# Eight changes of order and of PSUM banks at TensorE's waiting places in a two-block transformer kernel

## The chip, the cores and the metric

One NeuronCore of a Trainium2 chip runs the whole program. The metric is the time on the device in microseconds (us), the median of several executions; the profile is one further execution, taken by the hardware profiler. TensorE (PE) multiplies, VectorE (DVE), ScalarE (ACT) and GpSimd (POOL) work on tiles in SBUF (the first two also on PSUM, where PE writes), SyncE (SP) issues most of the transfers.

## The reference

256 tokens of width 1024 in float32 go through two transformer blocks. The first has a conditioning (six vectors of 1024 from `silu(c) @ w_ada`, with a bias), one attention that keeps the best keys of an indexer, one stick-breaking attention, and a layer of experts of which all 16384 rows of `u` and `v` are read. The second has a mixer of a short convolution, a block attention and a gated linear attention (GLA), a cross attention to a memory of 256 tokens, and a gated feed-forward layer of width 2752. Cut to what the change touches:

```python
mod = (cond @ w_ada[l] + b_ada[l]).reshape(b, 6, d)
shift1, scale1, gate1, shift2, scale2, gate2 = [mod[:, i] for i in range(6)]
hn = modulate(rmsnorm(x, norm1_g[l]), shift1, scale1)
...
suffix = lax.cumsum(log_one_minus, axis=3, reverse=True) - log_one_minus
a = jnp.where(strict, jnp.exp(log_beta + suffix), 0.0).astype(v.dtype)
...
hn2 = modulate(rmsnorm(x, norm2_g[l]), shift2, scale2)
f = peer_ffn(hn2.reshape(b * s, d), peer_wq[l], peer_sub_keys[l], peer_u[l], peer_v[l]).reshape(b, s, d)
x = x + gate2[:, None, :] * f
```

## The kernel before

The weights pass once through the core in **units** of 128 x 1024 floats (512 KB), in the order that `stream_plan` writes down (L204 on): w_ada (raw, for the conditioning), w_qi to w_vb, then w_qa to w_pb with a w_ada unit behind each, w_pa, w_o, w_pq, 128 units of u, 128 of v, and the second block's w2_*, w_up and w_dn. SyncE fetches them into 13 slots. ScalarE copies a unit's high half (`split`, L1298, type fp32r), and VectorE (L1834) or GpSimd (L2625) makes the low half, the rest to float32; `on_pool` in `stream_plan` says which of the two. A product takes three matmuls (`mm3`): high by high, high by low, low by high. There are three to eight buffers for split units, so an engine can be ahead of PE by two to six units, and every wait is a semaphore.

Each engine has a program of its own in the same order (`tensor_program`, `scalar_program`, `vector_program`, `gpsimd_program`). The products are `lin` (blocks of two column tiles in one bank, all steps of the first column before the second, unless `both`), `lin_nat` and `one`. Work that runs beside the products is a generator in `jobs`: each call of `unit` takes one step (one `yield`) of the first three jobs left, and `jobs.finish()` runs all that is left at once. All engines must keep to the same order of steps.

A PSUM bank is taken by `claim(b)`, which waits for the semaphore in `freed[b]`, that is for its last reader. `block_banks` hands out the banks of products, and `attention_banks` those of scores ("s") and transposes ("t").

- **Conditioning.** VectorE adds the w_ada units up in `ada_acc` (L1866, L1869), a group of 8 units for each of the six vectors. `ada_total` on PE then sums over the partitions with one-column matmuls, in bank 6 but for the second group, and `mod_part` on VectorE (L1850) adds the bias. It is called at the first w_ada unit after a group is complete, on both engines; the third group is gate1, which w_o needs, and the sixth is summed behind `total(1)`, ahead of w_pq.
- **Stick-breaking attention** (`stick_steps`): two waves of four heads; the cumulative sums are products with a triangle of ones, in banks 6, 7, 6, 7. VectorE adds them (L2125), and GpSimd masks before (L2702) and after (L2707). The value products take banks 6 and 7.
- **Attention** (`attend`): scores of two items at a step, soft maxima on VectorE (L1970, L1973) and ScalarE (L1412), transposes on PE (L787) in the same bank as the item's scores, values in banks 2 and 3. Scores of items 2 and 3 are issued one step ahead of the transposes of items 0 and 1, into the same banks 4 and 5.
- **Router.** After each block of w_pq (banks 4, 5, 6; the first is in bank 6) `key_scores` is a job of two steps. `jobs.finish()` ends the list behind the last block.
- **v stage.** Beside it the memory's normalisation (L1920, L1390, L2652) goes as a job, and the coefficients are made by ScalarE (L1637) and VectorE (L2373).
- **Second block.** w2_lr (the 16 columns of the gate) comes behind w2_mv and the start of the second attention; GLA's steps start behind it and wait for its copy (ScalarE, L1317). GpSimd makes the low halves of the normalised tiles (L2652), and takes its share of low halves of units only after them.
- **w_dn.** `lin` with 22 steps for each column; step k waits for `f_lo` k + 1, the low half of act_t (L2594).

## Time and profile before

| | us |
|---|---|
| median of 3 runs | 1443.64 |
| lowest and highest | 1441.86, 1446.01 |
| span of the profiled execution | 1450.8 |
| its PE busy | 1402.9 (97%) |
| its VectorE busy | 1097.6 (76%) |
| its ScalarE busy | 836.6 (58%) |
| its GpSimd busy | 358.2 (25%) |

The span is that from the first to the last instruction of the profiled execution; nothing that the profile shows lies outside it, and no other time of that execution is given, so the span stands for it, 7.2 us above the median. A matmul's end in the profile is modelled: matmuls overlap, so a busy PE can still be one that runs at half clock. So both are to be read: the idle time before an instruction, in brackets with the engine and line that ended it, and the granted clock (PEclk, a share of 2.4 GHz; 0.5 is 1.2 GHz).

### The profile page before, as it was taken

The page shows a single profiled execution, that of the slowest core. Times are in us where ns is not written, and L with a number is a line of the kernel's source. Part 1 is how long each engine was busy: PE and PEld are TensorE (multiplying, and loading weights), DVE is VectorE, ACT ScalarE, POOL GpSimd, SP SyncE. Part 2 cuts the span into 40 slices and gives each one's busy share as a digit, 9 for nine tenths or more (in the row PEclk, how much of TensorE's full clock was granted, in tenths as well). Part 3 has the DMA queues.
Part 4 walks back from the last instruction along what each step waited for, and adds up shares of the span by engine and source line. Part 5 has one row for each costly group of instructions (what it writes and reads, how often), then busy time and mean ns, then how long its engine had stood idle before and what let it go on. Part 6 is the DMA issues. An engine that isn't in the chain of part 4 may idle for free.

```text
span 1450.8 us, 25879 instructions
## 1 busy us (share of the span) xinstructions
PE 1402.9 (97%) x10406; PEld 1303.3 (90%) x10406; DVE 1097.6 (76%) x1903; ACT 836.6 (58%) x1447; POOL 358.2 (25%) x227
## 2 busy tenths in 40 slices
PE   7999999899999999999999999999999999899997
PEld 5998899799999999999988888887889899799997
DVE  6788887467889888999766666777667667787762
ACT  3554774444454577777654454465446666766651
POOL 3216101234345100000032322344322221433200
PEclk9999999999999999999999999999999999999999
DMA  9757775445655444444456666665666535275530
GB/s 383 270 187 268 248 240 176 160 150 187 187 182 162 155 151 148 148 150 148 146 188 220 196 192 193 217 191 183 190 205 244 180 115 189 81 252 177 191 116 30
DMA packets 73721, 268.24 MB, mean 185 GB/s; under 512 B 8401, under 2 KB 9730, under 8 KB 72834
## 3 DMA queue, kind: packets, MB, share of 16 engines
q1 hardware_dynamic: 71280, 256.41, 54.0%
q10 hardware_dynamic: 1426, 7.56, 1.5%
q0 software_dynamic: 896, 2.62, 0.5%
q8 instruction: 83, 1.36, 0.4%
q14 instruction: 36, 0.29, 0.1%
HBM read 262.88 MB, written 3.67 MB: 184 GB/s over the span
## 4 chain that ended last, share of the span: by engine, by line
PE 80%; DVE 13%; ACT 4%; DMA 1%; POOL 1%; issue 1%; DVEq 0%; ACTq 0%; POOLq 0%
PE bank L611 79%; DVE split L1834 3%; DVE ada_acc L1869 2%; DVE PR L2284 1%; DVE PR L2281 1%; ACT split L1298 1%; DMA ringb<-in_w_ada 1%; DVE PR L2289 1%; POOL H L2652 0%; DVE rT L1920 0%; PE bank L787 0%; POOL split L2625 0%; DMA vecs<-in_vecs 0%; DVE H L2373 0%; DVE PA L2085 0%
## 5 line engine op out<-in xcount | busy, mean ns | idle before, releaser
L611 PE MATMUL bank<-H,split 128*128 128x256 f32 x5928 | 736.3, 283 | 17.1 <-DVE split L1834 7.1
L611 PEld LDWEIGHTS bank<-H,split 128*128 128x128 f32 x5928 | 713.8, 190 | 24.1 <-DVE split L1834 9.4
L1298 ACT CAST split<-ringb 128x1024 fp32r<-128x1024 f32 x350 | 365.8, 1047 | 288.6 <-PE bank L611 278.4
L611 PE MATMUL bank<-split,H 128*128 128x512 f32 (+1 forms) x1728 | 390.9, 387 | 1.7 <-POOL split L2625 1.5
L2625 POOL TENSOR_TENSOR split<-ringb,split 128x1024 fp32r<-128x1024 f32 x91 | 225.4, 2478 | 670.4 <-ACT split L1298 670.4
L1834 DVE TENSOR_TENSOR split<-ringb,split 128x1024 fp32r<-128x1024 f32 x259 | 327.6, 1268 | 77.7 <-ACT split L1298 77.5
L611 PEld LDWEIGHTS bank<-split,H 128*128 128x128 f32 x1728 | 320.9, 188 | 69.8 <-POOL split L2625 2.5
L2373 DVE TENSOR_TENSOR H<-PR,H 128x256 fp32r<-128x256 f32 x128 | 137.3, 1074 | 106.3 <-ACT H L1637 106.2
L1834 DVE TENSOR_TENSOR split<-far,split 128x1024 fp32r<-128x1024 f32 x77 | 99.8, 1304 | 33.4 <-ACT split L1298 33.2
L1298 ACT CAST split<-far 128x1024 fp32r<-128x1024 f32 x89 | 92.9, 1047 | 53.2 <-PE bank L611 44.0
L1613 ACT ACTIVATE PR<-bank 128x512 f32<-128x512 f32 (+31 forms) x59 | 28.6, 486 | 75.9 <-PE bank L611 75.9
L2639 POOL TENSOR_TENSOR rT<-rT 128x256 f32<-128x256 f32 x25 | 26.7, 1067 | 177.2 <-ACT rT L1347 175.6
L611 PE MATMUL bank<-act_t,split 128*128 128x256 f32 x528 | 60.3, 276 | 0.8 <-DVE act_t L2594 0.8
L611 PEld LDWEIGHTS bank<-act_t,split 128*128 128x128 f32 x528 | 60.0, 188 | 1.0 <-DVE act_t L2594 1.0
L1596 ACT ACTIVATE xT<-cst,rT 128x128 bf16<-128x128 f32 x168 | 55.7, 438 | 0.0
L1637 ACT CAST H<-PR 128x256 fp32r<-128x256 f32 x128 | 51.2, 400 | 0.6 <-PE bank L611 0.6
L2346 DVE TENSOR_TENSOR PR<-bank,PR 128x224 f32<-128x224 f32 (+31 forms) x64 | 33.3, 520 | 23.6 <-PE bank L611 23.3
L2336 DVE TENSOR_TENSOR xT<-rt,cpw 128x512 bf16<-128x512 bf16 x126 | 45.8, 418 | 0.0
L2625 POOL TENSOR_TENSOR split<-far,split 128x1024 fp32r<-128x1024 f32 x12 | 31.1, 2591 | 58.5 <-ACT split L1298 58.5
L611 PE MATMUL bank<-Ym,split 128*128 128x256 f32 x336 | 41.2, 281 | 1.5 <-DVE Ym L1995 1.5
L611 PEld LDWEIGHTS bank<-Ym,split 128*128 128x128 f32 x336 | 39.7, 188 | 2.4 <-DVE split L1834 1.7
L611 PE MATMUL bank<-xT 128*128 128x128 bf16 x504 | 36.2, 219 | 0.0
(298 smaller groups left out, 1265.0 us busy)
## 6 DMA issues: line engine op xcount, KB each, us to landing
ringb<-in_u SPq DMA_DIRECT2D x128, 512.0 KB, 3.6
ringb<-in_v SPq DMA_DIRECT2D x128, 512.0 KB, 4.2
ringb<-in_w_ada SPq DMA_DIRECT2D x28, 512.0 KB, 5.3
far<-in_w_up SPq DMA_DIRECT2D x26, 512.0 KB, 4.2
far<-in_w_ada SPq DMA_DIRECT2D x20, 512.0 KB, 5.1
ringb<-in_w_up SPq DMA_DIRECT2D x17, 512.0 KB, 4.9
ringb<-in_w_pq SPq DMA_DIRECT2D x16, 512.0 KB, 3.7
far<-in_w_dn SPq DMA_DIRECT2D x14, 512.0 KB, 4.0
```

The source lines that it names most:

```text
L611: return TE.matmul(o, l, r, start=start, stop=stop, skip_group_check=True)
L1298: S.copy(buf(m)[0], slots[P.slot[m]]).then_inc(hi_done, 1)
L1596: S.activation(z[:, i // 2, :, i % 2], iota, ACT.Abs, bias=cpn[:, 4 * g + i:4 * g + i + 1]).then_inc(t_abs, 1)
L1613: ins = S.activation(d[:, :, n:T], o[:, :, n:T], ACT.Gelu)
L1637: S.copy(cf[i % 8][0], P3[:, i, :]).then_inc(c_hi, 1)
L1834: V.tensor_tensor(lo, slots[P.slot[m]], hi.bitcast(F32), ALU.subtract).then_inc(lo_v, 1)
L1869: V.scalar_tensor_tensor(out=acc, in0=w, scalar=cond[:, k:k + 1], in1=acc, op0=ALU.mult, op1=ALU.add).then_inc(ada_done, 1)
L2336: ins = V.tensor_tensor(t_gate[g % 3][:, z, :, :, :], t_col[g % 2], of_four(gp[:, 2 + z, :], g), ALU.mult)
L2346: V.tensor_tensor(d[:, 0:n, :], o[:, 0:n, :], d[:, 0:n, :], ALU.mult).then_inc(t_out, 1)
L2373: V.tensor_tensor(lo, P3[:, i, :], hi.bitcast(F32), ALU.subtract).then_inc(c_lo, 1)
L2625: G.tensor_tensor(lo, slots[P.slot[m]], hi.bitcast(F32), ALU.subtract).then_inc(lo_g, 1)
L2639: G.tensor_tensor(acc, acc if k > 1 else rT[:, square_row(q, 0), :], rT[:, square_row(q, k), :], ALU.add).then_inc(sq_add, 1)
```

## The change

Eight edits, all of order or of place; the arithmetic is the same, and no instruction of a compute engine is added or taken away.

1. The third conditioning group is summed six w_ada units later (`summed_after`), and the cumulative sums of the first wave take banks 6, 7, 4, 5, those of the second 6, 7, 2, 3 (`cum_bank`).
2. The transposes of attention items 0 and 1 take banks 6 and 7.
3. The sixth conditioning sum takes bank 3 (`ada_bank`).
4. `jobs.finish()` behind w_pq is gone on PE and ScalarE; the last `key_scores` runs beside the first units of u.
5. The low halves of the units v 92 and v 95 are VectorE's and not GpSimd's (`busy`).
6. w2_lr comes ahead of w2_mv, in the plan and on every engine; by the list of blocks, the two banks of w2_mv change places.
7. The low half of w_up's unit 4 is VectorE's (`busy`).
8. In the first block of w_dn the last step of column 0 comes behind the first two of column 1; the first matmul of column 1 then doesn't set the start flag.

```diff
-    for nm, k in [("w2_mq", 3), ("w2_mk", 4), ("w2_mv", 4), ("w2_lr", 1), ("w2_gk", 2), ("w2_gv", 2),
+    for nm, k in [("w2_mq", 3), ("w2_mk", 4), ("w2_lr", 1), ("w2_mv", 4), ("w2_gk", 2), ("w2_gv", 2),
...
+    busy = [P.at["v", 92], P.at["v", 95], UP0 + 4]
+
     def on_pool(i):
-        if i in first or O0 <= i < UP0 or i >= DN6:
+        if i in first or i in busy or O0 <= i < UP0 or i >= DN6:
             return False
...
     for it in range(16):
-        out[it, "s"] = out[it, "t"] = 4 + it % 2
+        out[it, "s"] = 4 + it % 2
+        out[it, "t"] = 6 + it if it < 2 else 4 + it % 2
...
-            return 3 if g == 1 else 6
-
+            return 3 if g in (1, 5) else 6
+
+        def summed_after(g):
+
+            return 6 if g == 3 else 0
+
+        cum_bank = ((6, 7, 4, 5), (6, 7, 2, 3))
...
             def ada_total():
                 g, pending = divmod(st["ada"], 8)
-                if pending or g == st["sum"]:
+                if pending != summed_after(g) or g == st["sum"]:
                     return
...
+                    steps = [(j, k) for j in range(2) for k in range(kt)]
+                    held = name == "w_dn" and p == 0
+                    if held:
+
+                        steps[kt - 1:kt + 2] = [(1, 0), (1, 1), (0, kt - 1)]
+                    for j, k in steps:
...
+                        o = (2 * p * kt + j * kt + k) % 8 * 128
...
+                        last = mm3(banks[b][:, j * T:(j + 1) * T], (wh[:, o:o + 128], wl[:, o:o + 128]), rhs(k),
+                                   k == 0 and not (held and j), k == kt - 1)
...
-                        o = claim(6 + i % 2)
+                        o = claim(cum_bank[w][i])
...
-                        freed[6 + i % 2] = (k_suf, h + 1)
+                        freed[cum_bank[w][i]] = (k_suf, h + 1)
...
             lin("w_pq", 16, hk, normed(1), both=True, after_block=lambda c: jobs.start(key_scores(c)))
-            jobs.finish()
...
             lin("w2_mk", 4, hk, mh, both=True, alone=4)
+            one("w2_lr", hk, mh)
             lin_nat("w2_mv", hkt, mh, 512)
...
             jobs.start(attend(ATT_M, need_m, lambda: t.wait_ge(*evac("w2_mv", 1))))
-            one("w2_lr", hk, mh)
```

ScalarE and VectorE follow with the same orders, and `mod_part` of the third group is called at the same unit as PE's sum.

## Rows read from the trace of the kernel before

**Rows 1.** The page, part 1: busy us, share of the span, instructions

```profile
PE 1402.9 (97%) x10406; PEld 1303.3 (90%) x10406; DVE 1097.6 (76%) x1903; ACT 836.6 (58%) x1447; POOL 358.2 (25%) x227
```

**Rows 2.** Waits of PE: who ended them, us in total, times, longest

```profile
PE bank L611 <- DVE split L1834: 7.1, 6, 2.4
PE bank L611 <- DVE mod L1850: 5.7, 2, 5.4
```

**Rows 3.** Timeline, 96 to 132 us: start, us, what, [idle before <-who]

```profile
114.36 1.92 PE L611 MATMUL bank<-zbuf,cst 128*128 128x256 f32 x12
...
120.54 2.75 PE L611 MATMUL bank<-cst,ada_acc 128*128 128x1 f32 x16 [1.07 <-DVE zbuf L2125]
...
123.55 3.78 PE L611 MATMUL bank<-PA,cst 128*128 128x256 f32 x12 [0.26 <-DVE mod L1850]
```

**Rows 4.** Windows: stretch, length, busy us (instructions), then PEclk, DMA share, GB/s

```profile
120.54:127.00 6.46, 6.20 (x29) 5.76 (x29) 3.37 (x5) 3.60 (x4) 2.35 (x5) 0.57 0.70 258
...
155.90:189.60 33.70, 31.48 (x260) 29.10 (x260) 33.35 (x54) 25.91 (x48) 7.61 (x8) 1.00 0.70 225
...
265.87:277.21 11.34, 11.34 (x74) 11.34 (x75) 1.81 (x2) 2.63 (x4) 1.98 (x1) 0.74 0.34 117
...
1267.05:1274.50 7.45, 7.45 (x50) 7.45 (x51) 7.02 (x10) 5.50 (x8) 2.82 (x2) 0.77 0.87 302
```

**Rows 5.** Timeline, 127 to 157 us: the fourth conditioning sum

```profile
154.02 1.84 PE L611 MATMUL bank<-cst,ada_acc 128*128 128x1 f32 x16
...
155.90 0.17 DVE L1850 TENSOR_TENSOR mod<-bank,vecs 128x8 f32<-128x8 f32 x1 [4.33 <-PE bank L611]
```

**Rows 6.** Timeline, 155 to 192 us: second wave, first transposes, fifth sum

```profile
170.74 2.02 PE L611 MATMUL bank<-PA,cst 128*128 128x256 f32 x12 [0.76 <-DVE zbuf L2125]
...
180.15 0.44 PE L787 MATMUL bank<-cst,PA 128*128 128x128 f32 x2 [0.58 <-DVE PA L1970]
...
181.47 0.44 PE L787 MATMUL bank<-cst,PA 128*128 128x128 f32 x2 [0.88 <-DVE PA L1970]
...
191.52 0.17 DVE L1850 TENSOR_TENSOR mod<-bank,vecs 128x8 f32<-128x8 f32 x1 [1.91 <-PE bank L611]
```

**Rows 7.** Timeline, 258 to 300 us: the start of w_pq

```profile
260.48 0.48 DVE L1924 SCALAR_TENSOR_TENSOR H<-rT,mod,H 128x256 fp32r<-128x256 f32 x1
...
265.87 11.33 PE L611 MATMUL bank<-H,split 128*128 128x256 f32 x72 [5.43 <-DVE mod L1850]
...
266.05 1.23 DVE L1834 TENSOR_TENSOR split<-ringb,split 128x1024 fp32r<-128x1024 f32 x1 [0.29 <-ACT split L1298]
...
277.84 5.90 PE L611 MATMUL bank<-H,split 128*128 128x256 f32 x48
```

**Rows 8.** Timeline, 316 to 326 us: behind the last block of w_pq

```profile
320.96 1.13 PE L611 MATMUL bank<-PR 128*128 128x128 f32 x8 [0.77 <-ACT PR L1317]
```

**Rows 9.** Timeline, 972 to 1016 us: the units v 92 to v 95

```profile
994.11 8.50 PE L611 MATMUL bank<-split,H 128*128 128x512 f32 x36 [0.74 <-POOL split L2625]
...
1003.31 12.99 PE L611 MATMUL bank<-split,H 128*128 128x512 f32 x56 [0.71 <-POOL split L2625]
```

**Rows 10.** Timeline, 1093 to 1156 us: behind w2_lr

```profile
1144.43 0.48 PE L611 MATMUL bank<-PB 16*128 16x128 f32 x2 [0.99 <-ACT PB L1317]
...
1145.51 4.61 PE L611 MATMUL bank<-H,split 128*128 128x256 f32 x24
...
1146.84 1.28 ACT L1714 ACT_TABLE_LOAD   x1
```

**Rows 11.** Timeline, 1244 to 1290 us: the start of w_up

```profile
1254.55 1.04 ACT L1298 CAST split<-far 128x1024 fp32r<-128x1024 f32 x1
...
1259.96 0.48 DVE L1920 SCALAR_TENSOR_TENSOR rT<-xT,vecs,bank 128x256 f32<-128x256 f32 x1 [0.22 <-POOL H L2652]
...
1267.05 23.12 PE L611 MATMUL bank<-H,split 128*128 128x256 f32 x181 [2.31 <-POOL split L2625]
```

**Rows 12.** Timeline, 1378 to 1396 us: the first block of w_dn

```profile
1387.03 9.13 PE L611 MATMUL bank<-act_t,split 128*128 128x256 f32 x78 [0.79 <-DVE act_t L2594]
```

## What I predict, and why

> **What bounds the kernel now.** I read the page first: TensorE (PE) is busy 1402.9 of 1450.8 us [rows 1], so what can be won is its 48 us of idle time and the stretches in which its clock is at half. Next the waits of PE alone: the largest that the change could reach are those on VectorE's low halves, 7.1 us in 6 places, and those on VectorE's sum `mod`, 5.7 us in 2 [rows 2]; a wait on one engine can stand for several places, so each edit is then looked up in the timeline, and what the stall does to the clock in the table of windows. Times below are from the start of the profiled span.
>
> **Part 1, cumulative sums and the third conditioning sum** (`cum_bank`, `summed_after`). At 119.5 PE has finished the first unit of w_va. It then needs bank 6 for the third `ada_total`, and bank 6 is held until VectorE has read the first cumulative sums out of it: 1.07 us idle, then 16 one-column matmuls in 2.75 us, 0.26 us idle for `mod`, then heads 2 and 3 of the cumulative sums in 3.78 us, where heads 0 and 1 took 1.92 [rows 3]. The granted clock of 120.54 to 127.00 is 0.57, that is nearly all at 1.2 GHz [rows 4]. After the change heads 2 and 3 have banks of their own (4 and 5) and follow at once: 119.5 + 1.9 = 121.4 in place of 127.0, 5.6 us earlier, and the rest of the half-speed stretch, some 1.3 us of it, is another 0.6. The sum itself isn't saved but paid six `w_ada` units later, where such a sum costs 1.84 us [rows 5]. What is late next is GpSimd's masking for the value products, about 0.5 us by its instructions in that timeline. So 5.6 + 0.6 - 1.84 - 0.5 = **3.9 us**, of which 6.46 x 0.43 = 2.8 is clock. Ends: 1.3 (the stalls alone) to 4.7. The moved sum makes VectorE wait for TensorE at a second place two units ahead of the one where it now idles 4.33 us [rows 5]. Behind that wait stand the low half of the next unit, an `ada_acc` addition and a step of the stick job; by their durations in that timeline (1.2, 1.3, 2.0, 1.2, 0.8) VectorE needs about 6.5 us to be back at the next sum, and TensorE needs two units of 2.9 and a sum of 1.84 [rows 5], 7.6. It costs nothing as long as this 1.1 us holds. `ada_acc` for group five must also wait for the later third sum, but that addition lies behind the same wait.
>
> **Part 2, second wave and the first transposes.** In the second wave the same reuse of bank 6 costs 0.76 us, and transposes 0 and 1 of the attention wait 0.58 and 0.88 us for `L1970`, because their bank is that of the scores of items 2 and 3 [rows 6]. With banks 2 and 3 for the sums and 6 and 7 for the transposes these go: **2.2 us**. The probabilities that the transposes read are ready two microseconds before. Low end: VectorE is busy 33.35 of 33.7 us in 155.9 to 189.6 [rows 4] and can't be hurried; but at 191.5 it waits 1.91 us for TensorE [rows 6], so 1.9 of the 2.2 is covered. From there to 236 VectorE starts when TensorE's sum is done, as now.
>
> **Part 3, the sixth conditioning sum in bank 3.** The first block of w_pq has bank 6, and so has this sum; VectorE adds it only after the whole normalisation, so PE stands 5.43 us though the first normalised tile is there at 260.96 [rows 7]. Then it runs three units in 11.33 us at a granted clock of 0.74 [rows 4, 7]; at full clock two take 5.90, that is 0.118 a matmul and a tail. With bank 3, PE starts at 261.0, goes at VectorE's pace (0.79 us for a tile, PE needs 6 x 0.118 = 0.71) and ends block 0 at 265.7 + 0.7 = 266.4. The next unit's low half is made at 266.05 to 267.28 [rows 7]: 0.9 us idle. The third unit ends at 267.3 + 2.9 = 270.2 in place of 277.2: **7.0 us**. If the clock still falls for as long, 11.34 x 0.26 = 2.9 less, so 4.1 to 7.0.
>
> **Part 4, no `jobs.finish()` after w_pq.** PE waits 0.77 us for ScalarE's copy of the last queries [rows 8]; now the first unit of u lies between. **0.8 us**; the routing on VectorE asks for these scores some ten units later. Ends 0 and 0.8.
>
> **Part 5, low halves of v 92 and v 95 on VectorE.** PE waits 0.74 and 0.71 us for GpSimd [rows 9]. VectorE and ScalarE hand the memory's normalisation and the coefficients to and fro in that stretch: a low half of 1.2 us [rows 7], a normalised tile, ScalarE's two copies of 0.4 and the coefficient make some 3.1 us a unit (estimate from that timeline) against PE's 2.7. So part of the stall becomes one for VectorE: **0.9 us** of 1.45. Ends -0.5 (two low halves of 1.2 us on VectorE, half of them seen) and 1.45.
>
> **Part 6, w2_lr ahead of w2_mv.** Now the gate product waits 0.99 us for the copy of w2_lr and the clock falls behind it: 24 matmuls in 4.61 us [rows 10] in place of 24 x 0.118 and the last one's tail of 0.16, 3.0, together 2.6 us. With four units between, this wait is gone. But the attention job starts one unit later against the gate job, so that exponentials, logarithm and exponentials again, with three table loads of 1.28 us [rows 10], follow each other on ScalarE while VectorE waits for the logarithm; by these durations the second transpose waits some 1.1 us. **1.5 us**, ends -1.5 and 2.6. The last heads are still out over 7 us before w2_o asks for them.
>
> **Part 7, low half of w_up 4 on VectorE.** GpSimd makes it only after its eight normalisation tiles, and PE waits 2.31 us; VectorE has ended its own at 1260.4 and its input was ready before [rows 11]. It does it at 1260.5 to 1261.7, while it would wait for ScalarE. So the stall goes, and with it the clock: 50 matmuls in 7.45 us at a granted clock of 0.77 [rows 4] against 50 x 0.118 = 5.9 at full clock, 1.6 more. **3.9 us**, low end 2.3.
>
> **Part 8, the first block of w_dn.** PE waits 0.79 us for the last low half of act_t [rows 12]; the first two steps of the second column, 6 matmuls or 0.71 us, now go between. The order of the other steps and the count of the weights is the same. **0.7 us.** As two sums are now open in one bank, the second one's first matmul no longer sets the start flag, which costs nothing.
>
> **The sum.** 3.9 + 2.2 + 7.0 + 0.8 + 0.9 + 1.5 + 3.9 + 0.7 = 20.9 us on the profiled execution's 1450.8. The median of the unprofiled runs is 1443.64, 7.2 below this span, and they lie 4 us apart. Some of that could be half-speed stretches which the profiled one had and they had not, so I take off one of 3.4 us, that is 1.7 us: 19.2, and 1443.6 - 19.2 = **1424.4 us** (-1.3%).
>
> **The rivals.** *The clock stays down.* 7.5 us of the sum is clock (2.8, 2.9, 1.6 and rounding). In part 3 PE still has 0.6 us of idle time behind one-column matmuls, and pauses remain at parts 1 and 7. If none of it comes back the gain is 13.4 and the time 1430.2. For it: after 120.5 the clock fell behind a stall of 1.07 us only [rows 3, 4]. Against it: it didn't fall at 154, behind a one-column sum without a stall [rows 5]. The Trainium skill, TensorE: Matmul & The Clock Gate, Part 1, says that the gate looks at activity on a free-running basis, so that the same kernel shows other cold stretches in another run; by that rule each of these stretches may come and go, which gives any time between the two. No row of a single execution can show this.
>
> *VectorE takes it back.* It is busy 33.35 of 33.7 us ahead of the sum at 191 [rows 4], and it gets two more waits (part 1), three more low halves (parts 5, 7) and the crowded start of the second attention (part 6). If parts 1, 2, 5 and 6 keep only their low ends (1.3, 0.5, 0, 0), the rest is 1.8 + 7.0 + 0.8 + 3.9 + 0.7 - 1.7 = 12.5, so 1431; with the clock rival on top, 1437.
>
> *The order is changed but the time isn't.* Each stall could only be the place where an earlier shortage shows. It would have to hold for parts 3 and 7 too, where the releasing engine idles or works on something else. 1443 +- 4.
>
> *Slower.* The moved third sum chains VectorE to TensorE right before the units where it has no slack [rows 4]. If it comes out of the two waits more than the 4.33 us late that it now idles [rows 5], every one of the 13 w_g units from there on has its low half late; from 1.9 us a unit on (24.7 us in all) the loss passes the gain of the other parts. It takes a VectorE that needs 6.1 us a unit where its 33.35 us over 8 units [rows 4] are 4.2; time from 1449 on.
>
> **Chances.** The forecast case, 1416 to 1429: 0.60. Clock stays down, about 1430: 0.14. VectorE takes back, about 1431 to 1438: 0.14. No change: 0.07. Slower: 0.04. More than forecast (the stalls at 449 and 475, which the change doesn't touch, may lose or keep their half-speed stretches): 0.01. The range 1415 to 1434 holds about 0.82. 0.3% is 4.3 us, about what a measurement of this kernel can tell from no change: faster 0.89, same 0.07, slower 0.04.
>
> **What would show it.** In the profile after: PE's waits on `mod` near 0 and no idle time of 5 us before w_pq, but a first block paced by `L1924`; bank sums 0 to 3 in one piece before w_va's second unit, and a one-column sum between the third and fourth w_g units; no wait of PE on GpSimd's split, and one on VectorE's under 0.5 us near the v stage's unit 95; no wait on the copy of w2_lr, and a new one of about 1 us at the third or fourth unit behind w2_mv; w_up's third block right behind its second. The prediction is wrong if PE is idle for more than 4 us between 120 and 236 (part 1's chain), or if half-speed stretches stay at w_pq and w_up.

## The result

The kernel after takes 1434.89 us (median of six runs, 1433.84 to 1437.43), and that before 1447.93 (median of six, 1441.86 to 1453.23): a recorded ratio of 0.9922, with a 95% interval of 0.9895 to 0.9948. Over all runs of this study it is 1447.5 +- 0.3 us for before (mean of 102 runs and its standard error) against 1435.9 +- 0.5 for after (18 runs): **11.6 us**. Forecast were 1424.4 us and a gain of 19.2, with a range of 1415 to 1434: the sign was right, the size too large, and the time lies just outside the range. (The gap to the forecast, 11.5 us by the means, is 7.6 us of gain that didn't come and 3.9 us of a base that was taken too low.)

The profiled execution of after took 1435.57 us, its span is 1433.8. First the page, part 1 (busy us, share, instructions), which answers to [rows 1], and the waits of PE (releaser, us in total, times, longest), which answer to [rows 2]:

```profile
PE 1396.7 (97%) x10406; PEld 1297.6 (90%) x10406; DVE 1094.9 (76%) x1906; ACT 836.1 (58%) x1447; POOL 356.3 (25%) x224
...
PE bank L619 <- DVE split L1845: 5.8, 5, 2.4
PE bank L619 <- POOL H L2663: 3.2, 5, 0.7
...
PE bank L619 <- ACT PA L1436: 1.4, 1, 1.4
PE bank L619 <- ACT PB L1329: 1.2, 1, 1.2
PE bank L619 <- POOL zbuf L2718: 1.1, 1, 1.1
...
PE bank L619 <- ACT PB L1436: 0.9, 1, 0.9
```

The waits on `mod` (5.7 us) are gone as foreseen. In their place stand four waits that before didn't have at these places: on the mask (`L2718`), on two ScalarE copies of transposed tiles (`L1436`), and on one of a product (`L1329`). That on GpSimd's normalisation tiles (`L2663`) has grown, from 1.1 us in all to 3.2.

Now the places. The start of w_va and the third sum, timeline of after (start, us, what, [idle before <-who]); answers to [rows 3]:

```profile
128.93 1.46 PE L619 MATMUL bank<-zbuf,PA 128*64 128x256 f32 x8 [1.06 <-POOL zbuf L2718]
...
141.72 1.84 PE L619 MATMUL bank<-cst,ada_acc 128*128 128x1 f32 x16
...
143.59 0.17 DVE L1861 TENSOR_TENSOR mod<-bank,vecs 128x8 f32<-128x8 f32 x1 [5.19 <-PE bank L619]
...
178.34 0.88 PE L619 MATMUL bank<-zbuf,PA 128*64 128x256 f32 x8 [1.40 <-ACT PA L1436]
```

The sum costs the 1.84 us again that were reckoned, VectorE waits for it, and nothing is late behind it. But the mask costs 1.06 us and not 0.5, and at 178.34 PE waits 1.40 us for the copy of the very transposes whose own waits (0.58 and 0.88, [rows 6]) went. The windows of after (stretch, length, busy us of PE, PEld, DVE, ACT, POOL, then PEclk, DMA share, GB/s), which answer to [rows 4], and the start of w_pq, which answers to [rows 7]:

```profile
120.54:127.00 6.46, 6.46 (x29) 5.19 (x28) 6.46 (x8) 3.55 (x4) 2.97 (x3) 1.00 0.91 328
...
252.00:263.00 11.00, 11.00 (x63) 10.46 (x63) 8.58 (x21) 5.09 (x10) 0.00 (x0) 0.69 0.52 186
...
253.08 2.91 PE L619 MATMUL bank<-cst 128*128 128x256 f32 x6
255.42 6.75 PE L619 MATMUL bank<-H,split 128*128 128x256 f32 x41
```

At w_va the clock holds. At w_pq the idle 5.43 us are gone, but in this execution the clock still falls, at 252.06, and the filler products `keep_busy`, which both kernels have there to bridge the gap, run at half rate into the first block.

Last, w2_mv to w_up, where two steps failed. Here PE waits for two copies that stand behind the second attention's exponentials on ScalarE, and at the start of w_up three times for a normalisation tile of GpSimd, whose eight tiles take 8.56 us in place of 6.63 before. (For before see [rows 10, 11] and the first line here; the others are of after.)

```profile
1257.08 6.63 POOL L2652 TENSOR_TENSOR H<-rT,H 128x256 fp32r<-128x256 f32 x8 [5.20 <-ACT H L1390]
```

```profile
1138.19 2.99 PE L619 MATMUL bank<-split,H 128*128 128x256 f32 x24 [1.16 <-ACT PB L1329]
...
1145.65 1.30 PE L619 MATMUL bank<-PB 64*128 64x128 f32 x16 [0.89 <-ACT PB L1436]
...
1242.95 8.56 POOL L2663 TENSOR_TENSOR H<-rT,H 128x256 fp32r<-128x256 f32 x8 [5.19 <-ACT H L1402]
...
1246.22 1.35 DVE L1845 TENSOR_TENSOR split<-far,split 128x1024 fp32r<-128x1024 f32 x1
1247.73 3.19 DVE L1845 TENSOR_TENSOR split<-far,split 128x1024 fp32r<-128x1024 f32 x2 [0.16 <-ACT split L1310]
...
1248.21 0.97 PE L619 MATMUL bank<-H,split 128*128 128x256 f32 x6 [0.69 <-POOL H L2663]
1249.89 0.97 PE L619 MATMUL bank<-H,split 128*128 128x256 f32 x6 [0.70 <-POOL H L2663]
1251.57 1.69 PE L619 MATMUL bank<-H,split 128*128 128x256 f32 x12 [0.70 <-POOL H L2663]
```

### The profile page after: what moved, and what is told of

Its sections match the earlier page's. It is cut to its first block, busy times and chain, and to the rows that moved or that the text cites. A ratio compares the mean times of both kernels' runs of the same rounds, so it can differ in the third digit from the quotient of the medians.

```text
span 1433.8 us, 25878 instructions
## 1 busy us (share of the span) xinstructions
PE 1396.7 (97%) x10406; PEld 1297.6 (90%) x10406; DVE 1094.9 (76%) x1906; ACT 836.1 (58%) x1447; POOL 356.3 (25%) x224
## 3 DMA queue, kind: packets, MB, share of 16 engines
q1 hardware_dynamic: 71280, 256.41, 56.4%
## 4 chain that ended last, share of the span: by engine, by line
PE 81%; DVE 12%; ACT 3%; DMA 1%; POOL 1%; issue 1%; DVEq 0%; POOLq 0%; ACTq 0%
PE bank L619 81%; DVE split L1845 3%; DVE ada_acc L1880 2%; DVE PR L2295 1%; POOL H L2663 1%; DVE PR L2292 1%; DMA ringb<-in_w_ada 1%; DVE PR L2300 1%; ACT split L1310 1%; DMA ringb<-in_w_g 0%; PE bank L800 0%; ACT PB L1424 0%; DMA vecs<-in_vecs 0%; DVE PA L2096 0%; DVE MH L1947 0%
## 5 line engine op out<-in xcount | busy, mean ns | idle before, releaser
L2636 POOL TENSOR_TENSOR split<-far,split 128x1024 fp32r<-128x1024 f32 x11 | 27.3, 2482 | 57.1 <-ACT split L1310 57.1
```

Source lines behind the costliest of these rows:

```text
L2636: G.tensor_tensor(lo, slots[P.slot[m]], hi.bitcast(F32), ALU.subtract).then_inc(lo_g, 1)
```

## How the traces were made comparable

Single executions of one kernel differ by up to 14 us here, more than any part is worth, so the first question was what differs. PE's time was cut at the same finished units in every trace, and in each piece three things were added up from the records of the matmuls: the **idle time** before a matmul, the **half-speed** loss (half of the time that was run in stretches with a granted clock of 0.5), and the **pace**, that is what the even stream of matmuls with 128 or 256 columns took over 113.3 ns apiece. What is left is the same in each trace of a program. Eighteen traces were cut like this: those of the two kernels above and of the sixteen runs below. Units are counted as PE finishes them, without those of w_ada. Length of each piece less its pace part, in us:

```
piece                      part  without the part                      with it
start, units 0 to 24        -    before 112.46 111.96 111.78 111.18    12 traces 110.9 to 111.3, 2 at 111.9, 112.0
w_va to w_g, 24 to 37       1    54.63 53.11 51.51 54.62 52.91         13 traces 51.03 to 51.16
second wave, 37 to 44       2    34.01 34.01 34.01 33.91 33.91         13 traces 32.59 to 32.70
w_pq, 59 to 75              3    63.10 62.80 62.89 63.15 62.17         57.96, 12 traces 56.27 to 56.40
u, 75 to 203                4    409.05 408.86 409.00 409.19 408.91    13 traces 406.39 to 409.49, mean 408.05
v, 203 to 331               5    352.10 352.06 352.03 352.10 352.08    13 traces 350.94 to 351.00
w2_mq to w2_o, 331 to 366   6    8 traces 123.79 to 127.06, mean 125.8 10 traces 125.8 to 128.0, mean 127.0
  of it, up to w2_mk             8 traces 38.2 to 40.3, mean 39.8      10 traces 38.1 to 40.3, mean 39.3
  of it, behind w2_mk            six 85.5 to 85.7, two 87.0, 87.1      10 traces 87.7 to 87.9
w_up, first units, 377-381  7    16.68 14.88 16.66 13.70 16.68         10 traces 14.27 to 14.48
w_dn, 420 to 443            8    67.20 66.92 66.92 66.95 66.94         13 traces 66.21 to 66.53
```

Where a column spreads without the part, it is mostly the half-speed stretch behind a stall, which comes in some executions and not in others; up to w2_mk it is a wait for one low half, and at w_up also GpSimd's tiles, of both of which more below. In the whole program, three traces of before lose 14.6, 9.2 and 9.3 us to it, their idle time is 30.6, 30.1 and 30.7; three of after lose 6.6, 3.5 and 3.3, and are idle for 20.6, 22.3 and 20.9.

## The experiments

**The kernel before again**, for what differs between two of its traces. 

> The kernel before, unchanged, for a second trace of the same program. Theory A (the gap between the profiled time of 1452.6 us and the three runs shown, 1441.9 to 1446.0, is made of half-speed stretches that come and go with the small stalls): the second trace has other half-speed stretches than the first, at three or more of the places 32.7, 121.5, 264.9, 449.2, 476.5, 1145.5 and 1268.4, and the difference of the two spans is the sum of the differences at those places, in steps of 1.5 to 3.5 us. Theory B (the whole program drifts, through the DMA or the engines' own pace): the same stretches stand in both traces and the difference is spread over the stages in pieces under 0.5 us.

Measured: 1448.17 us median of ten runs. Its profiled execution was the fastest of them (1443.07), 9.5 us below the one that the prediction was made from, whose time was 1452.6. Windows of this trace at the third sum and at w_up, which answer to the first and the last of [rows 4]:

```profile
120.70:127.20 6.50, 6.24 (x27) 5.42 (x27) 5.13 (x7) 2.85 (x3) 1.12 (x2) 0.74 0.74 250
...
1263.27:1270.72 7.45, 7.45 (x65) 7.45 (x66) 7.02 (x10) 5.48 (x8) 2.82 (x2) 1.00 0.87 301
```

Theory A holds in part: the stretch at w_va is half as long (0.74 against 0.57), and that behind the 2.31 us stall of w_up isn't there at all (1.00 against 0.77, 65 matmuls in the same 7.45 us in place of 50), nor is that at w2_lr. So the same stall, to a hundredth, draws a half-speed stretch in one execution and none in another. But only 5.5 of the 9.5 us are that, and 0.5 are idle time. Another 3.6 is something that neither theory had, the pace. Windows of 50 us inside w_up, where PE never waits: before, then before again, then after:

```profile
1300.00:1350.00 50.00, 50.00 (x427) 50.00 (x426) 39.73 (x66) 33.28 (x54) 14.44 (x6) 1.00 0.59 185
```

```profile
1300.00:1350.00 50.00, 50.00 (x444) 50.00 (x443) 41.30 (x67) 33.96 (x57) 15.14 (x7) 1.00 0.62 192
```

```profile
1300.00:1350.00 50.00, 50.00 (x427) 50.00 (x426) 40.33 (x66) 32.67 (x54) 14.49 (x6) 1.00 0.61 190
```

The same matmuls, no idle time, the same granted clock, and 444 of them in one trace where the other two have 427: 113.3 ns against 117.8 from start to start.

**A third trace of before.** 

> The kernel before, unchanged, a third trace. In nine traces so far the idle time of PE is a property of the program and the rest is drawn anew: half-speed stretches cost 14.6 and 9.2 us in the two traces of before, and the matmuls of w_up went at 117.9 ns apiece in the one and at 113.3 in the other, 3.7 us apart over that stage. Theory (the record of the prediction was a bad draw of before): idle time 30.1 to 30.6 us again; half-speed part 8 to 12 us, below the 14.6 of the first. Rival (14.6 is usual for before): 13 us or more; then the gain of the change in clock is real and something else ate it.

Idle 30.7 us and a half-speed part of 9.3: the theory holds, the 14.6 of the trace that the prediction was made from was a bad draw, 3.6 us above the mean of the three. In w_dn this trace has the slower pace where the first had the faster. Windows of w_dn, before and then this one, with a DMA share of 0.00 in both, so that it isn't the transfers:

```profile
1400.00:1430.00 30.00, 30.00 (x267) 30.00 (x266) 13.06 (x13) 10.48 (x13) 4.57 (x5) 1.00 0.00 1
```

```profile
1400.00:1430.00 30.00, 30.00 (x257) 30.00 (x256) 11.34 (x12) 8.69 (x11) 4.00 (x4) 1.00 0.00 1
```

**After again, twice.** 

> The kernel after, unchanged, for a second trace and more times on the chip of the three below. Theory, from the first six traces: PE's time splits into a part that is the same in all traces of a program, idle time (20.6 us in the first trace of after, 30.6 and 30.1 in two of before), half-speed stretches (6.6 us; 14.6 and 9.2 in the two of before), and a pitch of the matmuls that stands at 113.3 or 117.8 ns for long stretches (over 113.3 it cost 26.3 us; 25.5 and 21.8 in before). The second trace then has the idle time within 0.5 us of 20.6, while the half-speed part may differ by 1.7 us a stretch and the pitch part by up to 4 us. Rival: the idle time wanders as much as the rest, by more than 1.5 us.

> The kernel after unchanged, on the chip of the next. Idle time 20.6 to 22.3 us as in its two traces, mean time 1436.0 within 1.5 us. Over units w2_mq to w2_o 126.1 or 127.6 us without the pace, over w_up's first four units 14.4.

1436.8 and 1435.6 us (means of six runs each). Idle 22.3 and 20.9 us: the first is 1.7 above the first trace of after, just past the bound given to the rival. Of that, 0.7 lies at w_pq, where the clock held and PE so waits for tiles instead. Most of the rest is one wait of 1.22 us for the low half of w2_mk's last unit, which the first trace doesn't have (it has one of 0.65 us at another unit). Here are both, after_again and then the first trace of after:

```profile
1107.23 2.41 POOL L2636 TENSOR_TENSOR split<-ringb,split 128x1024 fp32r<-128x1024 f32 x1 [1.91 <-ACT split L1310]
1107.71 3.00 DVE L1845 TENSOR_TENSOR split<-ringb,split 128x1024 fp32r<-128x1024 f32 x1
...
1110.77 5.92 PE L619 MATMUL bank<-H,split 128*128 128x256 f32 x48 [1.22 <-DVE split L1845]
```

```profile
1108.73 1.23 DVE L1845 TENSOR_TENSOR split<-ringb,split 128x1024 fp32r<-128x1024 f32 x1
...
1108.93 3.29 POOL L2636 TENSOR_TENSOR split<-ringb,split 128x1024 fp32r<-128x1024 f32 x1 [2.60 <-ACT split L1310]
```

Of two low halves that overlap, the one that starts second takes longer, at this place in all seventeen traces in which they do overlap. In twelve, before among them, GpSimd starts 0.37 to 0.48 us ahead, VectorE's low half takes 3.0 to 3.1 us and PE waits 1.2 to 1.4. In five VectorE starts up to 0.23 us ahead and takes 1.23, GpSimd's takes 3.3 to 3.5, and PE doesn't wait. In the last, after_third, VectorE is done before GpSimd gets going. So idle time isn't quite a property of the program either. Units w2_mq to w2_o: 127.6 and 126.7; behind w2_mk they are alike, 87.7 in both.

**Part 3 undone.** 

> The kernel after with the sixth conditioning sum back in bank 6 (part 3 undone). The two traces so far put part 3 at 5.0 us, predicted were 7.0; the difference is the clock, which fell at 252.06 all the same. If the part acts by itself: PE waits about 5.4 us at the start of w_pq again and the time is 1434.9 + 5.0 = 1439.9 (1438.5 to 1441.5). Rival (without the stalls ahead of it the old order costs less, or w_pq's third unit hides it): under 3 us, 1437 or less.

```diff
-            return 3 if g in (1, 5) else 6
+            return 3 if g == 1 else 6
```

```profile
258.83 10.20 PE L619 MATMUL bank<-H,split 128*128 128x256 f32 x72 [5.43 <-DVE mod L1861]
```

1440.6 us, mean of ten, 4.7 above after. The stall is back to the hundredth (5.43 in [rows 7]). By the pieces the part is worth 62.8 - 56.5 = 6.3 us on the mean of 5 and 13 traces; this run's own trace has 62.17, and its times say 4.7 with a standard error of 0.7. In 10 of the 13 with it the clock holds; in two it falls for 3.41 us and the piece is no longer for it (56.4); only in the first trace of after did it fall for 6.83, and the piece take 58.0.

**The gap at w_pq filled.** 

> The kernel after, with two filler products in PE's idle 1.03 us at 248.9 (ahead of the squares of tiles 6 and 7) and four in place of three behind the sixth conditioning sum. Theory (the clock falls at 252.06 because PE was idle there just before): no half-speed stretch between 250 and 262, the first block of w_pq goes at full clock, 1.7 to 3.4 us less: 1431.5 to 1433.2 against after. Rival (the one-column products of the sum make it fall, or the pace of the first block): the stretch stays, somewhere from 252 to 256, and the time is the same; the fillers cost up to 0.3 us of it.

```diff
+                if q == 1:
+                    keep_busy(2)
                 for k in (6, 7):
...
-            keep_busy(3)
+            keep_busy(4)
```

```profile
252.00:263.00 11.00, 10.76 (x79) 9.93 (x80) 8.36 (x20) 7.32 (x12) 1.74 (x1) 1.00 0.51 180
```

No half-speed stretch, as expected; but after again has none either without the fillers, its window has 1.00 too, and w_pq takes 56.30 us here and 56.27 there. The time, 1435.8, is that of after. The stage is at its floor, the pace of the normalised tiles, as soon as the clock holds, so this run can't tell what made it fall in the first trace. Inconclusive for the cause, conclusive for the worth: nothing is left there but the draw.

**Parts 1 and 2 undone.** 

> The kernel after with parts 1 and 2 undone (cumulative sums in banks 6 and 7 alone, the third conditioning sum at its old place, transposes 0 and 1 in banks 4 and 5). The two traces so far put both at 4.7 us, 6.1 were predicted. If they act by themselves: the lead at w_o is 4.7 us less and the time 1439.6 (1438 to 1441), with the half-speed stretch at 121.5 back and the waits of 1.06 us (mask) and 1.40 us (copy of the transposes) gone. Rival (the slack ahead of the sum at 191 and the later chain on VectorE take most of it back): under 2.5 us, 1437.4 or less. What the clock does decides between the ends: without the half-speed stretch the stalls alone are 3.5 us less the 2.5 us of new waits.

```diff
-        cum_bank = ((6, 7, 4, 5), (6, 7, 2, 3))
+        cum_bank = ((6, 7, 6, 7), (6, 7, 6, 7))
...
-        out[it, "t"] = 6 + it if it < 2 else 4 + it % 2
+        out[it, "t"] = 4 + it % 2
```

(and the third sum behind its own eight units.) 1440.7 us, mean of ten, 4.8 above after, with a standard error of 1.0; its pieces give 1.8 for part 1 (52.91 against 51.1 us) and 1.3 for part 2 (33.91 against 32.6). Of part 2, the 0.76 us wait of the second wave's sums is back here and absent with the part in all 13 traces. Behind it, the kernel without part 2 is idle for 1.35 us and that with it for 1.40. The timelines of the two:

```profile
175.67 0.44 PE L800 MATMUL bank<-cst,PA 128*128 128x128 f32 x2 [0.47 <-DVE PA L1981]
176.99 0.44 PE L800 MATMUL bank<-cst,PA 128*128 128x128 f32 x2 [0.88 <-DVE PA L1981]
...
180.18 0.88 PE L619 MATMUL bank<-zbuf,PA 128*64 128x256 f32 x8
```

```profile
177.92 0.63 ACT L1436 COPY PA<-bank 128x256 f32<-128x256 f32 x2
...
178.34 0.88 PE L619 MATMUL bank<-zbuf,PA 128*64 128x256 f32 x8 [1.40 <-ACT PA L1436]
```

Undone, the transposes wait 0.47 and 0.88 and the value product doesn't; with the part, the transposes don't wait and the value product behind them waits 1.40, for ScalarE's copy, which stands in its queue behind the exponentials. One wait took the place of the other two; the copy itself comes at almost the same time in both (178.31 and 177.92).

**Parts 4, 5 and 8 undone.** 

> The kernel after with parts 4, 5 and 8 undone. By the traces of before and after they took 0.9 us (u), 1.35 (v) and 0.7 (w_dn) of idle time, and nothing came in its place: idle 20.6 + 2.9 = 23.5 us, time 1437.8 (1437 to 1439). Predicted were 0.8, 0.9 and 0.7. Rival (the v stage's gain is luck, or a new wait): v without idle time too.

```diff
+            jobs.finish()
...
-    busy = [P.at["v", 92], P.at["v", 95], UP0 + 4]
+    busy = [UP0 + 4]
...
-                    held = name == "w_dn" and p == 0
+                    held = False
```

1437.1 us (mean of six), 1.2 above after and so not clear of the scatter, and 24.1 us idle, 1.8 to 3.4 above the traces of after. The waits are back at all three places (0.8, 1.5 and 0.5 us): 408.91, 352.08 and 66.94 us for the pieces, against means of 408.05, 350.97 and 66.29. Together 2.6 us, and nothing new in their place.

**Part 6 undone.** 

> The kernel after with w2_lr back behind w2_mv (part 6 undone). By the first traces the part moved idle time rather than removing it: over the units of w2_mq to w2_o the time without half-speed stretches was 125.3 us in before and 126.1 in after. Theory: undone, PE waits 0.9 us for the copy of w2_lr again and the waits of 1.16 and 0.89 us on ScalarE's copies go; these units come out 0.4 to 0.9 us shorter, the time 1434.3 (same as after within its spread), a half-speed stretch at the wait included now and then. Rival (part 6 won what was predicted, 1.5 us): 1436.4.

```diff
-            one("w2_lr", hk, mh)
             lin_nat("w2_mv", hkt, mh, 512)
...
+            one("w2_lr", hk, mh)
```

(on all engines and in the plan.) 1433.9 us, mean of six, against 1436.8 for after on the same chip, a difference of 2.9 with a standard error of 1.2. The wait for the copy of w2_lr is back, and it is the only one in the start of the second attention:

```profile
1126.13 0.48 PE L619 MATMUL bank<-PB 16*128 16x128 f32 x2 [0.99 <-ACT PB L1329]
```

The piece takes 123.8 us here; over all traces it is 125.8 without and 127.0 with part 6. That mean mixes in the wait at w2_mk's last unit, which this trace doesn't have either and which stands ahead of everything that the part moves. Behind w2_mk the traces don't overlap where the clock holds: 85.5 to 85.7 us without, 87.7 to 87.9 with. The part **costs** 2.1 us there, 1.8 on the mean with the two half-speed stretches of the kernels without it: it removes a wait of 0.99 us and brings 1.16 and 0.89. About half of the 2.1 is this idle time; what the rest is was not looked into.

**Part 7 undone.** 

> The kernel after with the low half of w_up 4 back on GpSimd (part 7 undone). Theory (VectorE's low halves and GpSimd's eight normalisation tiles slow each other in the kernel after): without it the eight tiles take 6.6 us again in place of 8.56 and no tile over 0.9 us, the three waits of 0.7 us in w_up's first block are gone, the stall of 2.3 us ahead of the third block is back with its half-speed stretch, and the time is 1434.9 + 2.0 = 1436.9 (1436 to 1438). Rival (the slow tiles have another cause, such as the later place of the weights' transfers): the tiles stay slow and the time is 1434.9 + 3.9 = 1438.8.

1434.1 us, mean of six: no slower than after. Both theories are wrong in the number, the mechanism of the first is right:

```profile
1240.18 5.67 POOL L2663 TENSOR_TENSOR H<-rT,H 128x256 fp32r<-128x256 f32 x8 [5.20 <-ACT H L1402]
...
1248.23 3.10 PE L619 MATMUL bank<-H,split 128*128 128x256 f32 x24 [1.27 <-POOL split L2636]
```

The eight tiles are down from 8.56 to 5.67 us, with no wait of PE inside. VectorE paid meanwhile. Its two low halves of that stretch, from the view of one line's instructions (count: shortest, median, longest in ns, first and last start):

```profile
L1845 DVE TENSOR_TENSOR split<-far,split x2: 1210/3936/6662, 1245.0 to 1251.5; 128x1024 fp32r<-128x1024 f32 x2
```

One took 6.66 us in place of 1.21: it began at 1245.0 and ended at 1251.6, 1.1 us after GpSimd was done with its last tiles and, without a pause, its two low halves. So it stood behind several of GpSimd's instructions, and then took its own 1.2 us. When both engines are at it, one of them pays, and the order of the queues doesn't settle which: they are the same in before, where GpSimd was the one that paid (6.63 us for the tiles) and PE waited 2.31 us [rows 11] in place of 1.27.

**Part 7 kept, but VectorE held until GpSimd's tiles are made.** 

> The kernel after, with VectorE's low half of w_up 4 held back until GpSimd has made all eight normalisation tiles. Theory (the two engines slow each other when both read and write SBUF): the eight tiles take 5.7 to 6.6 us in place of 8.56, the three waits of 0.70 us at 1248 to 1251.6 go, the three low halves come between 1249 and 1253.5, before PE needs them at about 1253, 1256 and 1259; PE's idle time over w_up's first four units falls from 2.5 to 0.4 to 0.8 us, the time by about 1.9: 1433.0 against after. Rival (the tiles are slow by themselves, or the low halves come too late): the idle time stays at 2 to 2.5 us and the time at 1434.9; GpSimd's next low half may also be the one that loses, to 3.3 us instead of 2.4.

```diff
                             v.wait_ge(hi_done, P.hi_no[m])
+                            if m == P.at["w_up", 4]:
+                                v.wait_ge(n_lo, 8 * scaled_before(5) + 8)
```

```profile
1240.80 5.66 POOL L2665 TENSOR_TENSOR H<-rT,H 128x256 fp32r<-128x256 f32 x8 [5.20 <-ACT H L1402]
...
1247.85 3.09 PE L619 MATMUL bank<-H,split 128*128 128x256 f32 x24 [0.34 <-DVE split L1847]
```

The three waits of 0.7 us are gone, 0.34 and 0.24 come in their place, the piece takes 12.65 us in place of 14.4: the theory, in each of its numbers but the time. 1435.8 (mean of six) against 1436.8 on the same chip: 1.8 us can't be seen through runs that scatter by 2.

**Part 7 alone, on the kernel before.** 

> The kernel before with part 7 alone. The part was predicted at 3.9 us. By the traces so far its first four w_up units take 14.4 us in place of 13.7 to 16.7 (five traces with the stall, mean 15.7), and w_up goes at 117.8 ns a matmul in all nine traces that have the part, in place of 113.3 in two of five. Theory A (the part costs in pace what it gives in idle time): w_up at 117.8 ns, 14.4 us for the four units, and the time 1447.6 - 1.3 + 1.7, the same as before within 1 us. Theory B (the pace is drawn evenly): 117.8 or 113.3 ns, time 1446.3, 1.3 us less than before. Predicted by the step: 1443.7.

```diff
-        if i in first or O0 <= i < UP0 or i >= DN6:
+        if i in first or i == UP0 + 4 or O0 <= i < UP0 or i >= DN6:
```

1446.5 us (mean of twelve) against 1446.8 for before on the same chip: as theory A has it, though 1.3 us, theory B's gain, isn't excluded; it is 3.6 us short of the predicted 3.9. The tiles are at 8.58 us with PE waiting inside:

```profile
1255.88 8.58 POOL L2652 TENSOR_TENSOR H<-rT,H 128x256 fp32r<-128x256 f32 x8 [5.19 <-ACT H L1390]
...
1300.00:1350.00 50.00, 50.00 (x426) 50.00 (x426) 39.70 (x66) 32.70 (x54) 14.47 (x6) 1.00 0.58 185
```

w_up goes at the slower pace, as in all 13 traces with part 7 (held or not), while two of the five without it (before again, part 7 undone) had the faster.

**Parts 6 and 7 undone.** 

> The kernel after with parts 6 and 7 undone. Theory on idle time: w_up's first four units as with part 7 undone alone (2.0 us idle against 2.5 in after), the units of w2_mq to w2_o as with part 6 undone alone (1.5 us idle against 3.0 to 3.8 in after), so 1.9 us less idle than after. Theory on the pace: it is drawn where PE restarts last ahead of a long unbroken run. With the stall ahead of w_up's third block the pace was 117.9, 113.3 and 113.3 ns in three traces, with part 7 in place 117.8 in all seven. If the stall gives 113.3 more often, this kernel's w_up is at 113.3 and the time 1434.9 - 2 - 4 = 1429 in most runs, 1433 in the others; rival (the pace is drawn evenly whatever the order): the runs of this kernel and of the next have the same mean.

1435.6 us, mean of six, 1429.8 to 1439.9. Here the stall of w_up is 2.3 us again with its half-speed stretch (16.68 us for the piece), and w_up goes at 117.8 ns. The idle time, foreseen 1.9 us below after's, is 1.4 to 3.0 above it, by this stall and by some 2.4 us more in u. So the stall doesn't bring the faster pace by itself; it goes with it in two of five.

**One-column products put into w_up.** 

> The kernel after with one one-column product (two passes) ahead of w_up's blocks 3, 6, 9, 12, 15 and 18. Theory A (the pace of 113.3 or 117.8 ns is taken up where the even stream of matmuls is interrupted, and held from there): the pace changes at one or more of the six places, and w_up costs 106 us plus anything from 0.3 to 4.2 us and 6 x 0.2 us for the products. Theory B (the pace belongs to the operands or the stage): it stands at 117.8 ns from one end of w_up to the other, and the kernel is 1.2 us slower than after.

```diff
+                        if name == "w_up" and (j, k) == (0, 0) and p > 2 and p % 3 == 0:
+                            mm(banks[6][:, 0:1], ident, cst[:, 0:1], True, True)
```

1436.7 us (mean of four) against 1435.6 for after on the same chip. The pace is 117.8 ns before and after each of the six, to the end of w_up: theory B, as far as it goes. A break of 0.2 us without an idle PE doesn't change it. But the pace isn't a matter of operands or stage alone either, since the same code ran at both.

**Part 6 undone and VectorE held, twice.** 

> The kernel after with part 6 undone and VectorE's low half of w_up 4 held until GpSimd's tiles are made: the least idle time of what was seen, 19.2 - 1.5 = 17.7 us. Theory: idle 17.5 to 18.2 us, time 1434.9 - 1.5 (part 6) - 1.8 (held) = 1431.6. With w_up at 117.8 ns again it is no better than the kernel with parts 6 and 7 undone although it is idle for 1.0 us less.

> The kernel after with part 6 undone and VectorE's low half of w_up 4 held until GpSimd's tiles are made, again, beside after on one chip. Theory: 125.6 us over the units w2_mq to w2_o in place of 126.9 (mean of eight traces), 12.6 in place of 14.4 over w_up's first four: mean time 3.1 us below after, 1432.9. Rival (the account from traces misses what the times do): the two means within 1.5 us.

1432.1 and 1433.0 us, the second beside 1435.6 for after on one chip; together 1432.5 +- 0.7 (12 runs) against 1435.9 +- 0.5. Ratios to before 0.9888 (0.9861 to 0.9916) and 0.9897 (0.9877 to 0.9917). The pieces are as expected, 125.7 and 12.6 us; idle time is 21.5 in both and not 17.7, since u has 6.9 to 7.3 us here in place of 4.5, with one half-speed stretch less, a stretch that this edit doesn't touch. 3.4 us below after with a standard error of 0.9, the theory's 3.1. Beside after on one chip alone it is 2.7 with an error of 1.7, which doesn't exclude the rival's 1.5.

## Why the prediction was wrong, step by step

**The sum.** Measured by the pieces, next to what was predicted: part 1 2.3 (3.9), part 2 1.3 (2.2), part 3 6.3 (7.0), part 4 0.95 (0.8), part 5 1.1 (0.9), part 6 -1.8 (1.5), part 7 1.3 (3.9), part 8 0.7 (0.7): 12.2 us in place of 20.9. Add 0.6 at the start of the program, which the change doesn't touch, where there is a half-speed stretch in three of the four traces of before and of before with part 7, and in two of the 14 others, for no reason that was found; add 0.6 for the wait at w2_mk, and take off 1.5 for the pace (mean of its part 25.4 in three traces of before, 26.9 in three of after): 11.9, against 11.6 measured. That this is so close is partly luck: the pace's part alone lies 7 us apart in three traces of before. Nor can the times carry the split: those of the five runs that undo a part add up to 7.0 us over after, with an error of some 3.5.

**Part 7 failed**, and with it most of its term. The step "VectorE does it at 1260.5 to 1261.7, while it would wait for ScalarE" looked for a free engine and found one, but GpSimd was on its tiles just then (1257.1 to 1263.7). 8.56 us in place of 5.7 to 6.6 for these is what the idle VectorE's help cost, and PE waits for tiles instead of weights. The Trainium skill, SBUF — State Buffer, in its section on the two separate sides, calls the port pair that VectorE and GpSimd share "an **exclusive lock**, not a bandwidth split", held for a whole instruction, and names VectorE's operations with two inputs in SBUF among those that take it. The traces agree: 6.66 us for a low half of 1.21 in one, 8.56 for eight tiles of 5.67 in the other. It should have been a rival with a price of its own, and the trace of before had one to read, at w2_mk: VectorE's low half took 3.02 us beside one of GpSimd, and PE waited 1.24. The other half of the term, 1.6 us of clock, was the draw of one execution: of five traces with the stall, three have the half-speed stretch. The 1.3 us that are left of the part are nearly all the chance of that stretch. Where the clock held, the piece takes 14.88 and 13.70 us without the part and 14.3 to 14.5 with it.

**Part 6 failed** in sign. A stall of 1.1 us was foreseen at the second transpose. One of 1.16 came, but at a product that waits for ScalarE's copy, and another of 0.89 behind it was not in the sum; measured at a held clock the part costs 2.1 us. The 1.6 us of clock in the gain was again one draw: the stretch is there in two of the eight traces without the part.

**Part 2 failed in the half that is the transposes** (1.46 of its 2.2 us; the other 0.76, the bank of the second wave's sums, came): the waits of the transposes were reckoned gone and what is late next was looked for on VectorE 13 us later; it was the next copy on ScalarE, one instruction behind the transposes.

**Part 1** came to 2.3 of its 3.9 us. Its gain is nearly all clock, 2.0 us on the mean of five traces without it, where 2.8 was read off one. Of the stalls only 0.3 to 0.5 us is left, since the mask takes back up to 1.06 (0.5 was foreseen): before_third, without a half-speed stretch at w_va, takes 51.51 us where the kernels with the part take 51.1. **Part 3** held nearly whole: the clock cost something in one trace of 13. Parts 4, 5 and 8 came out within 0.2 us. The moved sum did no harm, as the margin of 1.1 us said. Of the signs named as fatal, idle time of over 4 us between 120 and 236 came just so (4.06 us), but through the mask and the copy, and 1.6 us of it, behind w_pb, stood there before; no wait in it is on the moved sum. The stretch at w_up went, that at w_pq stayed in the first trace.

**The base failed too.** 1443.6 was the median of three runs; 102 runs have a mean of 1447.5, so 3.9 us of the miss in the time lie here, and the 7.2 us between the profiled span and those three were read as a sign of stretches that may come and go, of which I took off one. The span doesn't stand for the time either: in the runs here the time of the profiled execution is 1.7 to 1.9 us above its span, and that of before was 1452.6. The rival "the clock stays down" has the right idea and the wrong form: the clock doesn't stay down, it falls by chance behind a stall. Priced as such, at its mean over executions, before loses some 11 us to it, not 14.6. (The 7.5 us of clock in that rival also left out the 1.6 us that part 6's gain held.) At w_va the three traces of before have a stretch of 6.83 us, of 3.41 and none, behind stalls of 1.07, 1.35 and 0.71 us, and take 54.63, 53.11 and 51.51 us. The prediction cites the Trainium skill, TensorE: Matmul & The Clock Gate, Part 1, for half-speed stretches that differ between runs of the same kernel; by these three traces it is so.

## What to carry over

- A stall that is taken away is worth what the next thing in line leaves of it: look first at the next instruction on the queue that released it, then further off. A helper engine is free only if those that share its way to memory are free too.
- What a half-speed stretch costs can't be read off one profile. Price it with a chance, and take the base from as many runs as there are: here the spread of one kernel (1439 to 1454) was larger than the gain.
- Cut the traces at the same finished units and count idle time, clock and pace apart. Parts worth 0.7 to 1.3 us were then clear in traces where six timed runs couldn't show 2.

## What the hardware showed

- **Two paces of the matmul.** Streams of 256-column matmuls at a granted clock of 1.00 run at 113.3 or 117.8 ns from start to start and keep it for over 900 matmuls; with the slower one the weight load begins 115 ns ahead of its matmul, with the faster 110. Over w_up that is 4 us, over w_dn 2. It isn't the transfers (DMA share 0.00 in w_dn), and a product of one column between them doesn't change it. What sets it is open; that part 7 does was not shown (13 of 13 traces slow with it, 3 of 5 without).
- **VectorE against GpSimd.** Of two low halves (1.2 us on VectorE and 2.4 on GpSimd when alone) the one that started second was the slow one in all seventeen traces in which they overlapped at w2_mk: VectorE's then took 3.0 to 3.1 us, or GpSimd's 3.3 to 3.5, while the first kept its time. Eight subtractions of 128x256 on GpSimd took 5.7 us with VectorE out of the way, 6.6 in before and 8.6 with VectorE's low halves among them; two such low halves took 7.8 us in the execution where GpSimd won.
- **Clock.** Behind a stall of 2.31 us, the same to a hundredth, the granted clock fell for 3.41 us in three traces and not at all in one. At w_va of the kernel before it fell for 6.83 us, for 3.41 or not at all in three executions.
